# Stationary high weights over both operand parts in one 512-column matmul, and seven pairs' weight sums made in the convolution stage

## What the kernel must compute

```
# layer 0: seven projections, two gated convolutions, one output projection
p = h @ w_in                                  # 2048 x 7168
ya = a_b * conv3(a_c * a_x);  yb = silu(layernorm(conv31(b_val * sigmoid(b_gate)) + bias))
x = x + rmsnorm(concat(ya * silu(a_z), yb * silu(b_z)) @ w_out)
# layer 1: pooling mixer
v, z = split(h @ w_in, 2)                     # 2048 x 4096: v and z of 2048 columns each
pooled = trailing_mean(v, windows 2/4/8/16 by group) - v
y = (per_group(pooled @ c_w) + c_b) * c_scale * silu(z)
x = x + rmsnorm(y @ w_out)
```

## Time and profile before

| | us |
|---|---|
| median of 3 executions | 1319.17 (1318.10 to 1319.45) |
| the profiled execution | 1319.22 |
| its span in the trace | 1317.4 |
| PE busy | 1305.6 (99%) |
| weight loads (beside PE) busy | 1130.0 (86%) |
| VectorE busy | 987.8 (75%) |
| ScalarE busy | 507.5 (39%) |
| GpSimd busy | 138.2 (10%) |
| granted TensorE clock | 0.998 of full |

### The profile page before, as it was taken

The page is one execution under the profiler, slowest core; times in us unless marked ns, Lnnn a source line. Parts: engine busy times, 40 slices in busy tenths (PEclk is TensorE's granted clock), DMA queues, the critical chain, the costliest instruction groups (busy, mean ns, idle before and its releaser), DMA issues. The chain is left out here.

```text
span 1317.4 us, 16646 instructions
## 1 busy us (share of the span) xinstructions
PE 1305.6 (99%) x6910; PEld 1130.0 (86%) x6910; DVE 987.8 (75%) x946; ACT 507.5 (39%) x557; POOL 138.2 (10%) x125
## 2 busy tenths in 40 slices
PE   9999999999999999999999999999999999999997
PEld 7888888888888888888888899899999999888886
DVE  6489998769755644544975887858878888799888
ACT  6521232221222121233565654234444445555552
POOL 0000000000007600000000100001213232000001
PEclk9999999999999999999999999999999999999999
DMA  9724443333357889761775564424434444764157
GB/s 323 224 65 112 112 114 108 90 101 96 96 162 240 256 260 293 229 225 41 268 294 195 188 180 128 133 73 118 130 110 126 139 132 158 258 223 160 46 211 255
DMA packets 234034, 219.75 MB, mean 167 GB/s; under 512 B 4016, under 2 KB 192560, under 8 KB 228976
## 3 DMA queue, kind: packets, MB, share of 16 engines
q1 hardware_dynamic: 227936, 208.42, 50.8%
q10 hardware_dynamic: 4512, 5.42, 1.2%
q0 software_dynamic: 1520, 4.98, 1.0%
HBM read 192.85 MB, written 25.95 MB: 166 GB/s over the span
## 5 line engine op out<-in xcount | busy, mean ns | idle before, releaser
L905 PE MATMUL bank<-h_hi,w_hi 128*128 128x512 f32 (+1 forms) x1536 | 545.6, 355 | 1.4 <-DVE w_lo L1671 1.0
L907 PE MATMUL bank<-h_lo,w_hi 128*128 128x512 f32 (+1 forms) x1536 | 543.8, 354 | 0.0
L909 PE MATMUL bank<-h_hi,w_lo 128*128 128x512 f32 (+1 forms) x1536 | 543.7, 354 | 0.0
L905 PEld LDWEIGHTS bank<-h_hi,w_hi 128*128 128x128 f32 x1536 | 290.8, 189 | 42.9 <-issue 1.8
L907 PEld LDWEIGHTS bank<-h_lo,w_hi 128*128 128x128 f32 x1536 | 290.8, 189 | 40.3 <-issue 0.7
L909 PEld LDWEIGHTS bank<-h_hi,w_lo 128*128 128x128 f32 x1536 | 290.8, 189 | 40.1
L1671 DVE TENSOR_TENSOR w_lo<-raw,w_hi 128x2048 fp32r<-128x2048 f32 x64 | 154.2, 2410 | 51.7 <-ACT w_hi L1200 51.6
L1200 ACT ACTIVATE w_hi<-raw 128x2048 fp32r<-128x2048 f32 x64 | 122.2, 1910 | 150.6 <-PE bank L909 131.3
L905 PE MATMUL bank<-w_hi,h_hi 128*128 128x512 f32 x448 | 174.6, 390 | 0.2 <-DVE rows L1950 0.2
L907 PE MATMUL bank<-w_lo,h_hi 128*128 128x512 f32 x448 | 174.3, 389 | 0.0
L909 PE MATMUL bank<-w_hi,h_lo 128*128 128x512 f32 x448 | 174.3, 389 | 0.0
(11 more groups left out here) (162 smaller groups left out, 1442.9 us busy)
## 6 DMA issues: line engine op xcount, KB each, us to landing
raw<-e_in SPq DMA_DIRECT2D x52, 1024.0 KB, 5.8
raw<-o_in SPq DMA_DIRECT2D x20, 1024.0 KB, 6.2
scratch<-e_out SPq DMA_DIRECT2D x17, 1024.0 KB, 7.2
spare<-e_out SPq DMA_DIRECT2D x12, 1024.0 KB, 7.5
rows<-o_in SPq DMA_DIRECT2D x12, 1024.0 KB, 6.0
spare<-o_out SPq DMA_DIRECT2D x12, 1024.0 KB, 7.3
scratch<-o_out SPq DMA_DIRECT2D x10, 1024.0 KB, 5.1
e_sums<-scratch SPq DMA_DIRECT2D x8, 1024.0 KB, 4.9
```

The lines of the kernel that those rows point to most:

```text
L905: nc.tensor.matmul(dst, w[0], m[0], start=first, stop=False, skip_group_check=goes_on)
L907: nc.tensor.matmul(dst, w[0], m[1], start=False, stop=False, skip_group_check=goes_on)
L909: return nc.tensor.matmul(dst, w[1], m[0], start=False, stop=last, skip_group_check=goes_on)
```

## The change

- `half_product` runs two matmuls in place of three for each of its eight 128-row parts: the high weights over high and low operand side by side (512 columns, into the whole bank), then the low weights over the high operand (256 columns, onto the first half). The bank's second half holds high by low.
- The high and low arrays are put into one tensor each (`h_both`, `w_both`, `t1_both`), so that one access pattern reads both.
- Each result is now the sum of a bank's two halves. So the kept copies are of 512 columns, and `v11`, `v12` and `z22_sum` are two dependent additions (512, then 256 columns). z21, which was read by the silu from the bank, needs a copy of one half by ScalarE (`copy_z21`), an addition by VectorE (`z21_sum`) and then the silu; the silu of z22 moves to behind S1 of the next pair.
- For the pairs 0, 2, 4, 6, 8, 10 and 11 (`EARLY`) the four weight sums are made by VectorE in the steps c = 1 to 7 of the convolution stage, from quarters loaded then, stored to DRAM (`pair_sums`) and loaded again, as forms, in the slab pairs. The five other pairs make their sums as before.
- All loads of the pairs are by halves of a slab (512 KB) in place of whole slabs, issued one by one as each form's buffer is split.
- VectorE at the start of the next stage, GpSimd before it overwrites the buffer, and SP before `load_term` wait until the sums are stored (`early_stored`).

```diff
+EARLY = (0, 2, 4, 6, 8, 10, 11)
+EARLY_FROM = 1
 def half_product(kind, p, dst, m, fresh):
                 for k in range(KH):
-                    last = product(dst, (hi[:, k * P:(k + 1) * P], lo[:, k * P:(k + 1) * P]),
-                                   (m[0][:, k * HALF:(k + 1) * HALF],
-                                    m[1][:, k * HALF:(k + 1) * HALF]),
-                                   fresh and k == 0, k == KH - 1, True)
+                    both = m[:, :, k * HALF:(k + 1) * HALF]
+                    nc.tensor.matmul(dst, hi[:, k * P:(k + 1) * P], both,
+                                     start=fresh and k == 0, stop=False, skip_group_check=True)
+                    last = nc.tensor.matmul(dst[:, 0:HALF], lo[:, k * P:(k + 1) * P],
+                                            both[:, 0, :], start=False, stop=k == KH - 1,
+                                            skip_group_check=True)
 # ScalarE
-                    nc.scalar.activation(p1, y, ACT.Copy).then_inc(p1_kept, 1)
+                    nc.scalar.activation(p1[:, :], y, ACT.Copy).then_inc(p1_kept, 1)
                 elif kind == S1:
                     act.wait_ge(form_done, f + 1)
-                    act.wait_ge(z22_ready, p)
+                    if p > 0:
+                        silu_z22(p - 1)
+                        act.wait_ge(z22_silu, p)
...
                     act.wait_ge(v12_ready, p)
+                    act.wait_ge(z21_silu, p)
+                    nc.scalar.activation(p1_p6[:, :], y, ACT.Copy).then_inc(p1_p6_kept, 1)
+            def copy_z21(p):
+                act.wait_ge(form_done, AT_FORM[X22, p] + 1)
+                act.wait_ge(v12_ready, p + 1)
+                nc.scalar.activation(z21, pair_bank(p, 0)[:, HALF:T], ACT.Copy)\
+                    .then_inc(z21_copied, 1)
+            def silu_z21(p):
+                act.wait_ge(z21_ready, p + 1)
+                nc.scalar.activation(silu_row(PLAIN + p)[:, 0:HALF], z21, ACT.Silu)\
+                    .then_inc(z21_silu, 1)
                 if kind == X22:
-                    silu_halves(p)
+                    copy_z21(p)
                 else:
                     keep(f)
                 if f + RING <= last_form:
                     form_high(f + RING)
                 if kind == X22:
+                    silu_z21(p)
                     silu_scaled(p)
 # VectorE (v11 and v12 likewise)
-                nc.vector.tensor_tensor(z22, p5, pair_bank(p, 0), ALU.add).then_inc(z22_ready, 1)
+                link(nc.vector.tensor_tensor(p5[:, :], p5[:, :], pair_bank(p, 0), ALU.add))
+                nc.vector.tensor_tensor(z22, z22, p5[:, HALF:T], ALU.add).then_inc(z22_ready, 1)
+            def z21_sum(p):
+                dve.wait_ge(z21_copied, p + 1)
+                nc.vector.tensor_tensor(z21, z21, pair_bank(p, 0)[:, 0:HALF], ALU.add)\
+                    .then_inc(z21_ready, 1)
+                elif kind == X22:
+                    z21_sum(p)
 # VectorE, convolution stage, for c = 1 to 7: four sums, i = c - 1
+                early_first(c)     # S1 and S3, ahead of L1792
...
+                early_second(c)    # S2, behind two more taps
...
+                early_third(c)     # S4, behind two more taps, ahead of split_ahead(c + 1, 0)
 # SP, convolution stage
+            def load_early(i):
+                if i == 0:
+                    sp.wait_ge(x_squared, TT)
+                else:
+                    sp.wait_ge(early_stored, 16 * 4 * i)
+                for kind in (S1, X22, X11, X12):
+                    sp.dma_start(early[kind].rearrange("p (k c) -> p k c", c=P),
+                                 pair_half(kind, EARLY[i])).then_inc(early_loaded[kind], 16)
+            def store_early(i):
+                for m, kind in enumerate((S1, S3, S2, S4)):
+                    sp.wait_ge(early_summed, 4 * i + m + 1)
+                    sp.dma_start(pair_sums[m, i], early_sum[kind]).then_inc(early_stored, 16)
 # SP, slab pairs: behind the split of each form of an early pair
+                    if kind == X11:
+                        load_form(S2, p)
+                    elif kind == S1:
+                        load_form(S4, p)
+                    elif kind == S2:
+                        load_form(X11, p + 2)
+                    elif kind == X12:
+                        load_form(X12, p + 2)
+                    elif kind == S4:
+                        load_form(S1, p + 2)
```

More of the change, by code:

```diff
@@ L113 @@
 AT_FORM = {form: n for n, form in enumerate(PAIR_FORMS)}
+EARLY = (0, 2, 4, 6, 8, 10, 11)
+EARLY_FROM = 1
+LATE = [p for p in range(PAIRS) if p not in EARLY]
+HALVES = ("v1", "v2", "z1", "z2", "s3")
 T_SUMS = {"y11": 1, "y12": 2, "t1": 3, "y22": 4, "t3": 5, "t2": 6, "y21": 7, "t4": 8}
@@ L197, in build @@
         sz = (sz0, sz1)
-        odd_taps = sz0
+        odd_taps = ln_rstd
+        early = {X11: scratch[:, 5 * T:7 * T], X12: scratch[:, 12 * T:14 * T],
+                 S1: scratch[:, 9 * T:11 * T], X22: scratch[:, 14 * T:16 * T]}
+        early_sum = {S1: early[X22], S3: early[S1], S2: early[X11], S4: early[X12]}
         x_tok = [scratch[:, n * T:n * T + D] for n in (2 * TT, 3 * TT)]
@@ L222, in build @@
         v_row, sum_a, sum_b = (shifted[:, n, :] for n in range(3))
-        p1, p5 = kept[:, 0, :], kept[:, 1, :]
-        p1_p6, z22 = sums[:, 0, :], sums[:, 1, :]
+        z21, z22 = p1_p6[:, 0:HALF], p5[:, 0:HALF]
         v_buffer = (raw[:, 0, :], rows[:, 0:4, :].rearrange("p a c -> p (a c)"))
@@ L295, in build @@
         t_lo_ready = sem("t_lo_ready")
-        v_pair_loaded = [sem(f"v_pair_loaded{n}") for n in range(2)]
-        z_pair_loaded = [sem(f"z_pair_loaded{n}") for n in range(2)]
+        early_loaded = {kind: sem(f"early_loaded{kind}") for kind in (X11, S1, X12, X22)}
+        early_summed = sem("early_summed")
+        early_stored = sem("early_stored")
+        half_loaded = {name: [sem(f"half_loaded_{name}_{n}") for n in range(2)]
+                       for name in HALVES}
         s1_summed = sem("s1_summed")
@@ L382, in ring, with form_home @@
             return w[:, slot, half * HALF_SLAB:(half + 1) * HALF_SLAB]
+        def form_home(kind, p):
+            return {X11: "v1", S2: "v1", X12: "v2", S4: "z1" if p in EARLY else "v2",
+                    S1: "z1", X22: "z2", S3: "s3"}[kind]
         def form_source(kind, p):
@@ L387, in form_source, with half_turn @@
             first, second = slice(0, HALF_SLAB), slice(HALF_SLAB, SLAB)
-            return {X11: v[:, first], S2: v[:, first], X12: v[:, second], S4: v[:, second],
-                    S1: z[:, first], X22: z[:, second], S3: s3_buffer}[kind]
+            return {"v1": v[:, first], "v2": v[:, second], "z1": z[:, first],
+                    "z2": z[:, second], "s3": s3_buffer}[form_home(kind, p)]
+        def half_turn(kind, p):
+            home = form_home(kind, p)
+            if home == "s3":
+                return sum(1 for e in EARLY if e <= p and e % 2 == p % 2)
+            twice = home in ("v1", "z1")
+            before = sum(2 if twice and e in EARLY else 1 for e in range(p % 2, p, 2))
+            return before + (2 if kind in (S2, S4) else 1)
         def pair_bank(p, n):
-            return bank[4 * (p % 2) + n][:, 0:HALF]
+            return bank[4 * (p % 2) + n][:, :]
         def plain_slab(s):
@@ L701, in _, with load_form @@
[L701 to L705, removed]
-            sp.wait_ge(t_lo_ready, T_SPLIT["t4"])
-            load_v(1)
-            for p in range(2, PAIRS):
-                pair_form_split(S4, p - 2)
-                load_v(p)
-                pair_form_split(X22, p - 2)
-                load_z(p)
+            def load_form(kind, p):
+                if p >= PAIRS:
+                    return
+                dst, loaded = form_source(kind, p), half_loaded[form_home(kind, p)][p % 2]
+                if kind in (X11, X12, X22) or (kind == S1 and p in LATE):
+                    sp.dma_start(dst.rearrange("p (k c) -> p k c", c=P), pair_half(kind, p))\
+                        .then_inc(loaded, 16)
+                elif p in EARLY:
+                    sp.dma_start(dst, pair_sums[(S1, S3, S2, S4).index(kind), EARLY.index(p)])\
+                        .then_inc(loaded, 16)
```

177 lines of the change are left out of this document (126 added, 51 removed).

## The result

The changed kernel takes 1322.56 us (median of 7 runs, 1321.91 to 1323.91), the kernel before 1319.09 (7 runs, 1318.10 to 1320.60): ratio 1.0029, 95% interval [1.0019, 1.0039]. It is slower by 0.3%, where 1317.0 and at most 1319.9 were forecast. The profiled execution took 1321.91 us, its span is 1320.1.

A forecast was written before the change was run, and what follows sets the result against it. PE, busy 99% at full clock, was taken to set the time by its own rate. 1319.22 - 8.96 + 4.4 + 2.4 = 1317.06, forecast 1317.0 us; own range 1315.3 to 1318.7, the wider range reaching into the 1312.6 case and up to 1319.9.

The forecast's parts named there:

- What PE saves: PE's half products in the slab pairs: a step falls from 360.0 to 346.7 ns, saving 8.96 us over 84 half products.
- steps of 512 columns over 230 ns: Sign that the forecast is wrong: PE's 512-column matmuls in the pairs take over 230 ns, where 227 was expected.
- The waits at X22: PE waits for z22 at X22 of pairs 2, 4, 6 and 8: 1.1 us each, 4.4 in all, bounds 0.5, 1.3.
- Pair 6's chain: ScalarE's silu of z21 waits for VectorE's z21_sum, so the P1+P6 copy starts 1.50 us behind S2, before 0.19.
- The start of the maps: After pair 11 the same ScalarE delay makes PE wait for pooled_low: 2.4 us with refill, bounds 1.9 and 2.7.
- The sums in the convolution stage: VectorE's four added sums in steps 1 to 7, 4.56 us a step, cost PE 0; bounds 0 and 3 us.
- VectorE's wait of 5.90 us for PE: In convolution step 5 this wait for PE's slab shrinks to 2 to 3 us; a sign of being right.
- z22's second half beside GpSimd: In late pairs z22's second addition loses 0.4 us more if GpSimd's window sums slow it like the low part.
- the rival that GpSimd holds z22 back: z22's second addition blocks until GpSimd's first window addition (1.66 us) ends: four stalls of 2.1, 1321.0 us; chance 0.07.
- That the waits don't arise: VectorE finds 1.1 us in odd pairs, leaving the map stall: 1312.6, chance 0.13; without that stall too 1310.3, 0.05.
- That the stored sums come too late: In early pairs reloaded sums land late, at 12.5 us transit: six pairs lose 2.6 us each, 1328; chance 0.07.
- The own range: The forecast's range for the whole kernel from its terms' bounds: 1315.3 to 1318.7 us.

The follow-up runs named there:

- e7_sums_only: The kernel before with only the weight sums of seven pairs moved into the convolution stage and pair loads by halves: 1318.88 us, ratio 0.9998.

## Why the prediction was wrong

**The step that failed is the size of "What PE saves".** It priced a step at 226.7 + 120.0 = 346.7 ns, each matmul as in a row of its own kind. By turns the two cost 353.3, in the kernel and by themselves, so 84 half products gave 84 x 0.053 = 4.5 us and not 8.96. That error alone, 4.5 us, moves 1317.0 to 1321.5. The check named for it ("steps of 512 columns over 230 ns") was the right one: they take 235. The other terms add up with it: 4.5 from PE's rate, 1.1 more of waits in the pairs (5.5 for 4.4), 0.1 less at the maps, 1.1 less ahead of the pairs and 0.5 more behind the first map matmul make 1317.1 + 4.9 = 1322.0 for the profiled execution, which took 1321.91; the median is 0.65 above it. That the result is not further off is in part luck, since the shorter time ahead of the pairs was in no term.

**The waits at X22**: place and mechanism right. The four came at pairs 2, 4, 6 and 8 as forecast, with 0.8, 0.8, 1.2 and 1.2 (and 0.1 each to refill) for 1.1 each with the refill, and the reordered ScalarE loop took them away. Pair 6's chain was 0.37 us later at ScalarE than forecast, as VectorE's low parts ahead of z21_sum lay beside GpSimd's window additions (3.20 us for two). With PE slower than thought (ready at T + 14.13, not 13.87) part of that was hidden. Not foreseen were 1.1 us of small waits at S4, S3 and X22 of pair 9.

**The start of the maps**: 2.2 and 0.1 to refill for 2.4, right; the reordering left 0.9 of the 2.2.

**The sums in the convolution stage**: cost 0, right; the changed kernel has no gap of PE there, and the moved sums alone make no difference (0.9998). One detail was wrong: VectorE's wait of 5.90 us for PE didn't shrink to 2 to 3, it is gone, and none for PE is left from 58 us to the end of the stage. A step keeps VectorE 41.6 us and some small waits for ScalarE, not 41.1, so its lead doesn't grow again, but it lasts.

**z22's second half beside GpSimd**: it took 0.71 us at pair 6 and 0.82 to 0.83 at the ten pairs before and behind it, for 0.43 at the last pair, where GpSimd is idle. 0.4 was allowed for. Where the time goes shows when GpSimd's additions are read one by one. For pair 6 the first of them, to be read beside VectorE's 1013.22 above; for pair 5 the second, with VectorE's low part; and the first in the kernel before, beside the low part of the earlier trace rows at 970.78:

```profile
1012.61 1.03 POOL L977 TENSOR_TENSOR shifted<-shifted 128x512 f32<-128x512 f32 x1 [4.67 <-issue]
...
992.61 1.10 POOL L977 TENSOR_TENSOR shifted<-shifted 128x512 f32<-128x512 f32 x1
992.74 2.06 DVE L2331 TENSOR_TENSOR w_both<-raw,w_both 128x1024 fp32r<-128x1024 f32 x1
...
970.68 1.03 POOL L879 TENSOR_TENSOR shifted<-shifted 128x512 f32<-128x512 f32 x1 [3.52 <-issue]
```

At pair 6 z22's addition ends at 1013.93, 0.29 us behind the end of GpSimd's (1013.64). At the ten others it begins 0.1 us earlier beside GpSimd's and takes 0.1 us longer: it ends 0.28 to 0.29 us behind the end of GpSimd's in all eleven. The low part at 992.74 ends 1.09 us behind GpSimd's second addition, that at 970.78 1.09 behind the first. All 21 VectorE instructions of 128x1024 with both inputs in SBUF that began beside a GpSimd addition in the pairs, 0.13 to 1.11 us into it, ended 1.08 to 1.09 us behind its end; alone they take 1.22. So the later one waits until the earlier one has ended. It holds the other way round too: a window addition begun behind a low part lasts 1.90 us for 1.03. An addition that reads a bank is not held: begun 0.09 us into a GpSimd addition it takes 0.42 us as alone (run e7_sums_only). The Trainium skill (SBUF — State Buffer, "Who interferes with whom") has the later of two such instructions fully block, and the trace agrees.

So the rival that GpSimd holds z22 back had the mechanism right, and the argument against it was a misreading: the low part of the earlier trace rows did wait for the end of GpSimd's first addition. Its price was wrong. It took a third of the three additions' 4.99 us, 1.66, for the first, which lasts 1.03, while the others last 1.90 since they are held up themselves; and half of the first is over when z22's second addition begins. It costs 0.3 to 0.4 us a pair and not 1.2. That its 1321.0 lies nearest to the result of all the times named is luck. The same block is the 0.85 us of the kernel without moved sums: one low part more that waits for a window addition.

**Rivals.** That the waits don't arise is refuted by the trace. That the stored sums come too late is too: ScalarE waits for them, but no X22 or S2 of an early pair makes PE wait for a transfer, and they land within 7.0 us. It is right only in the sign, for another reason. No rival had PE's rate itself as its mechanism, and the term had no bound: the rate of a mixture was taken from two uniform rows. Bounded below by no saving at all (360.0 ns a step as before), the range would have held the result. The own range was narrower than its terms besides: with 2.0 to 5.2 for the four waits, 1.9 to 2.7 for the maps and 0 to 3 for the convolution stage, the bounds give 1314.1 to 1321.1 and not 1315.3 to 1318.7. The result lies above these too.

## What to carry to other kernels

When a change turns a uniform row of matmuls into a mixture of widths, time the mixture by itself first, and where it costs, try the order high, low, low, high. A result that needs one more step on a second engine should not stand ahead of the copies and roundings which the next product waits for: moving two instructions in an in-order queue was worth 7 us here. A gain of PE's rate shows in the time only when no other engine's loop is the longer one, so remove the waits first and judge the rate then. And when an instruction beside another engine takes longer, compare its end with the end of each single instruction there, and not its length with a mean: only that tells a wait from a slowdown.

## What the runs showed of the hardware

- Matmuls of 512 and 256 columns by turns cost 353.3 ns a pair, for 347.1 in rows of their own; two and two 348.3. With 384 columns beside 512 the excess is 12.8 ns, beside 256 there is none.
- Narrow matmuls stop getting cheaper: 256 columns 120.0 ns, 192 and 128 between 111 and 112.
- A read of two runs of 256 costs the same as one of 512, and the bank that the short one writes makes no difference.
- A VectorE instruction with both inputs in SBUF that begins beside a GpSimd addition waits for its end: a 128x1024 one ends 1.08 to 1.09 us behind it (1.22 alone), a 128x256 one 0.28 to 0.29 (0.43 alone). One that reads a bank isn't held (0.42).
- At a granted clock of 0.5 matmuls of 512 and 256 columns cost 427 and 213 ns, in proportion to their columns; at full clock, with 227.1 and 120.0, they don't.
